# Gate products of the bidirectional layers: pairs of tiles with seven block products in place of eight, and a new order of the work around them

## The chip, the cores and the metric

The kernel runs on one core of one Trainium2 chip. The metric is the device time of one execution in microseconds. The times before are 2038.31 us as the median of three runs (2038.30 to 2046.05).

## The reference

The program is two stacks one after the other on 512 tokens of width 1024. What matters here is the end of each of the two layers of the second stack (`second_block`):

```python
h = _rms_norm(x, norm_g[l]); p = h @ w_in[l]
c_q, c_kv, k_pe, z_a, u_f, z_f, g_a, g_f = _split_in(p)        # g_a and g_f: 1024 columns each
o_a = _mla_branch(...)                                           # attention, 512 wide
y_a = (o_a * jax.nn.silu(z_a)) @ w_attn_proj[l]
y_f = (_fourier_branch(u_f) * jax.nn.silu(z_f)) @ w_fourier_proj[l]
m = (jax.nn.sigmoid(g_a + b_merge[l, 0]) * y_a
     + jax.nn.sigmoid(g_f + b_merge[l, 1]) * y_f)
x = x + m @ w_out[l]
```

## The kernel before, in words

Activations lie feature-major: a tile is 128 features by 512 tokens, eight tiles (`KT`) make the width. Every float32 product is made of three matmuls on split operands, `w_hi*x_lo + w_lo*x_hi + w_hi*x_hi` (helper `three`, matmuls at L870 to L872), so one 128-wide output tile over eight input tiles is 24 matmuls of 512 columns.

Weights come as a stream of 312 blocks of 128 x 1024 numbers (eight 128 x 128 tiles, 512 KB). `block` says which product uses which block. A block passes through: SP loads it into `raw` (three slots, `RING`), ScalarE rounds it to `w_hi` (L1594), GpSimd computes `w_lo = raw - w_hi` (L3113), TensorE uses it. ScalarE issues the rounding at places written out by hand in its program: `passed(key)` and `product(key)` call `weights(b + 2)`, where b is the key's last block. Each engine's program is written out in order; nothing is reordered at run time. PSUM has eight banks; `bank_filled`, `bank_read` and `block_used` hand them from TensorE to VectorE and ScalarE and back.

The multilayer perceptrons of the first stack already use seven products for eight (`seven`, matmuls at L975 to L977). The 1024 x 512 product of a pair of output tiles is cut in 2 x 2 blocks. From a weight block VectorE forms four sums of 128 x 256 (`weight_sums`, L2379 to L2384) in banks 4 and 5, after ScalarE has copied one quarter there (`w21`, L1610). ScalarE rounds the sums (L1621), VectorE subtracts (`weight_sums_lo`, L2390). Sums of the inputs (`t_hi`, `t_lo`) are formed once per layer. Half a pair, one block, is then 42 matmuls of 256 columns. Seven outputs of VectorE (L2466 to L2478) put the pair's two tiles together.

The end of a bidirectional layer, which changes, runs like this in the kernel before:

- TensorE: attention, then eight small products of the Fourier branch (`dd`, L1499 to L1502), then the products `f` (two blocks, four output banks, 48 matmuls). Then for m = 0 to 7: gate tile `ga` m, gate tile `gf` m, one block each, and `ya2` m and `yf2` m, four input tiles each, which share a block. Then eight tiles `out2`.
- VectorE: `d_lo` (L3028) for the eight `dd`; `of` g = `f` g * `z_f` (L3034) and its low part (`lo`, L2316), g = 0 to 3; for each m the gates times the norm's root (L3042), two products with the sigmoids (L3046), their sum (L3049) and its low part.
- ScalarE: `d_hi` (L2246), the silu of `z_f` (L2248), the rounding of two weight blocks, the high parts of `of` (L1683), then sigmoids (L2257) and weight blocks in turns.

Of the kernel before, what the change touches and what calls it, by code (L numbers as in the profile page):

```python
# [27 lines left out]
P = 128  # L28
T = 512
# [108 lines left out]
def stream_of(inp):  # L138
# [76 lines left out]
    for l in range(LAYERS2):  # L215
# [147 lines left out]

def plan_core():
# [62 lines left out]
    def mlp(layer):  # L427
# [8 lines left out]
        for part in range(1, FF_PARTS + 1):  # L436
            for g in range(2):
# [12 lines left out]
                for m in range(NT * g, NT * g + NT, 2):  # L450
# [78 lines left out]
    for l in range(LAYERS2):  # L529
# [29 lines left out]
        splits(*[("of", l, g) for g in range(FG)])
        for m in range(KT):  # L560
            each("ga", l, m, n=1)
            each("gf", l, m, n=1)
            gemm([("ya2", l, m), ("yf2", l, m)], 1, apart=True)
            splits(("m", l, m))
        each("out2", l, n=KT)
    sums = [block[key][0] + n for key in block if key[0] == "up" for n in range(2)]
# [7 lines left out]
def place(nc, c):  # L574
# [133 lines left out]
    c.m_hi, _ = put("m_hi", [P, KT, T], o, F32R)  # L708
    c.m_lo, _ = put("m_lo", [P, KT, T], o + 16384, F32R)
# [16 lines left out]
    c.sig, _ = put("sig", [P, 4, T], local)  # L726
# [4 lines left out]
    assert o <= tail, o - tail  # L731
    c.u_f, _ = put("u_f", [P, 4, T], a + 16384 + 8192)


def add_semaphores(nc, ctx, c):
# [26 lines left out]
    c.split_src = sem("split_src")  # L762
    c.split_hi = sem("split_hi")
# [75 lines left out]
def program_tensor(pe, nc, c, block, bank, split, beside, early, sum_blocks):  # L839
# [101 lines left out]
    def seven(layer, part, g, half):  # L941

        key, first = ("up", layer, part, g), (part, g) == UP_PAIRS[0]
# [4 lines left out]
        for n, (_, w, x) in enumerate(SEVEN):  # L948
            bnk, use, _ = bank[(*key, n // 2)]
            if half == 0 and n % 2 == 0:  # L950
                if use:
                    pe.wait_ge(c.bank_read[bnk], use)
                if first:
                    pe.wait_ge(c.split_lo, split[("a", layer, int(bnk < 2), bnk)] + 1)
                elif bnk % 2 == 0:
                    before = ("a", layer, part, bnk // 2) if g else ("a", layer, part - 1, 2 + bnk // 2)
                    pe.wait_ge(c.split_lo, split[before] + 1)
            out = c.psum[bnk][:, n % 2 * HALF:n % 2 * HALF + HALF]
            for k in range(2):
                i = 2 * half + k  # L960
                if first and x < X_11:
                    pe.wait_ge(c.split_lo, split[("t", 2 * layer + 1, i)] + 1)
# [17 lines left out]
            elif half and n % 2:  # L980
                ins.then_inc(c.bank_filled[bnk], 1)
# [2174 lines left out]
```

## Time and profile before

| what | value |
|---|---|
| median of three runs | 2038.31 us |
| profiled execution | 2038.94 us |
| its span, first to last instruction | 2037.0 us |
| TensorE busy | 2020.0 us, 99% |
| VectorE busy | 1166.9 us, 57% |
| ScalarE busy | 1007.8 us, 49% |
| GpSimd busy | 730.5 us, 36% |
| DMA | 179.19 MB, mean 88 GB/s |
| granted TensorE clock | 1.0 |

The profiled execution's span is its time but for 1.9 us around it. Busy time of TensorE is that of matmuls whose ends are modelled, and a matmul's shown duration overlaps the next one's start; what a matmul costs in a full stream is the distance between two starts. The same holds in part for VectorE and ScalarE: their instructions follow each other a little faster than they last.

### The profile page before, as it was taken

The numbers are of one execution on the slowest core, as the hardware profiler recorded it, in microseconds if no ns is written. First come the engines' busy times: TensorE is split into PE (matmuls) and PEld (weight loads), VectorE is DVE, ScalarE is ACT, GpSimd is POOL, SyncE is SP. The second block draws the span as 40 slices with busy tenths as digits, with TensorE's granted clock in tenths as the row PEclk, the third lists the DMA queues.
The fourth block names the chain that finished last, engine by engine and source line by source line (L and its number), as shares of the span: only waits on it lengthen the run. The fifth ranks groups of instructions, "written<-read, shape, count | busy, mean of one in ns | idle before, by whom it ended". The sixth has DMA issues, their size and how long they took to land.

```text
span 2037.0 us, 30204 instructions
## 1 busy us (share of the span) xinstructions
PE 2020.0 (99%) x12180; PEld 1663.9 (82%) x12180; DVE 1166.9 (57%) x1983; ACT 1007.8 (49%) x1655; POOL 730.5 (36%) x342
## 2 busy tenths in 40 slices
PE   8999999999999999999999999999999999999999
PEld 6777788989888886778898888878788887878887
DVE  6884566666647158863656564667733334774331
ACT  7752465444436328874544343566743344775221
POOL 3332144444444631004444444434044443402443
PEclk9999999999999999999999999999999999999999
DMA  4432123332232430002333232222022232201222
GB/s 160 133 131 72 47 97 104 103 104 96 103 104 91 145 96 32 1 16 93 104 104 104 100 108 94 93 80 87 2 93 93 95 101 84 83 22 63 93 97 89
DMA packets 62729, 179.19 MB, mean 88 GB/s; under 512 B 17776, under 2 KB 18160, under 8 KB 62592
## 3 DMA queue, kind: packets, MB, share of 16 engines
q1 hardware_dynamic: 47600, 168.04, 24.3%
q10 hardware_dynamic: 14992, 9.22, 1.7%
q8 instruction: 98, 1.61, 0.3%
q14 instruction: 39, 0.32, 0.0%
HBM read 171.97 MB, written 3.70 MB: 86 GB/s over the span
## 4 chain that ended last, share of the span: by engine, by line
PE 97%; ACT 1%; DVE 1%; issue 0%; DMA 0%; POOL 0%; DVEq 0%; ACTq 0%
PE banks L870 23%; PE banks L872 22%; PE banks L871 22%; PE banks L977 4%; PE banks L976 4%; PE banks L975 4%; PE banks L1362 2%; PE banks L1328 2%; PE banks L1341 2%; PE banks L1451 1%; PE banks L1464 1%; PE banks L1436 1%; PE banks L921 1%; PE banks L1442 1%; PE banks L1044 1%; PE banks L1236 1%
## 5 line engine op out<-in xcount | busy, mean ns | idle before, releaser
L3113 POOL TENSOR_TENSOR w_lo<-raw,w_hi 128x1024 fp32r<-128x1024 f32 (+4 forms) x338 | 730.3, 2165 | 1290.5 <-ACT w_hi L1594 1190.9
L1594 ACT ACTIVATE w_hi<-raw 128x1024 fp32r<-128x1024 f32 (+2 forms) x286 | 284.4, 994 | 453.6 <-PE banks L872 334.7
L870 PE MATMUL banks<-h_lo,w_hi 128*128 128x512 f32 (+1 forms) x992 | 401.0, 404 | 7.5 <-POOL w_lo L3113 7.5
L872 PE MATMUL banks<-h_hi,w_hi 128*128 128x512 f32 (+1 forms) x992 | 387.8, 391 | 0.0
L871 PE MATMUL banks<-h_hi,w_lo 128*128 128x512 f32 (+1 forms) x992 | 387.6, 391 | 0.0
L870 PE MATMUL banks<-a_lo,w_hi 128*128 128x512 f32 x768 | 304.4, 396 | 0.0
L872 PE MATMUL banks<-a_hi,w_hi 128*128 128x512 f32 x768 | 299.2, 390 | 0.0
L871 PE MATMUL banks<-a_hi,w_lo 128*128 128x512 f32 x768 | 299.2, 390 | 0.0
L2362 DVE TENSOR_TENSOR x<-x,banks 128x512 f32<-128x512 f32 x168 | 115.1, 685 | 213.4 <-PE banks L872 213.4
L870 PEld LDWEIGHTS banks<-h_lo,w_hi 128*128 128x128 f32 (+1 forms) x992 | 186.0, 187 | 54.4 <-POOL w_lo L3113 7.5
L871 PEld LDWEIGHTS banks<-h_hi,w_lo 128*128 128x128 f32 (+1 forms) x992 | 186.2, 188 | 41.8 <-issue 5.5
L872 PEld LDWEIGHTS banks<-h_hi,w_hi 128*128 128x128 f32 (+1 forms) x992 | 186.0, 187 | 40.9 <-issue 1.2
L870 PEld LDWEIGHTS banks<-a_lo,w_hi 128*128 128x128 f32 x768 | 144.1, 188 | 36.9 <-DVE x L2362 7.4
L872 PEld LDWEIGHTS banks<-a_hi,w_hi 128*128 128x128 f32 x768 | 144.2, 188 | 30.9
L871 PEld LDWEIGHTS banks<-a_hi,w_lo 128*128 128x128 f32 x768 | 144.2, 188 | 29.1 <-issue 1.0
L2390 DVE TENSOR_TENSOR w_lo_s<-banks,w_hi_s 128x1024 fp32r<-128x1024 f32 x52 | 63.5, 1220 | 88.8 <-ACT w_hi_s L1621 88.8
L2257 ACT ACTIVATE sig<-sig,params 128x512 f32<-128x512 f32 x32 | 23.1, 723 | 135.6 <-DVE sig L3042 135.6
L975 PE MATMUL banks<-t_lo,w_hi_s 128*128 128x256 f32 x312 | 86.1, 276 | 0.0
L976 PE MATMUL banks<-t_hi,w_lo_s 128*128 128x256 f32 x312 | 86.1, 276 | 0.0
L977 PE MATMUL banks<-t_hi,w_hi_s 128*128 128x256 f32 x312 | 86.1, 276 | 0.0
L3042 DVE TENSOR_TENSOR sig<-banks,norm 128x512 f32<-128x512 f32 x32 | 22.1, 692 | 104.1 <-PE banks L872 104.1
L1621 ACT ACTIVATE w_hi_s<-banks 128x1024 fp32r<-128x1024 f32 x52 | 52.9, 1018 | 35.7 <-DVE banks L2384 35.7
(423 smaller groups left out, 3760.0 us busy)
## 6 DMA issues: line engine op xcount, KB each, us to landing
raw<-in_weights SPq DMA_DIRECT2D x311, 512.0 KB, 3.2
x<-in_x SPq DMA_DIRECT2D x4, 512.0 KB, 5.9
AT<-row_dram ACTq DMA_DIRECT2D x4, 512.0 KB, 8.7
out<-x SPq DMA_DIRECT2D x8, 256.0 KB, 2.2
eg<-row_dram ACTq DMA_DIRECT2D x8, 128.0 KB, 3.1
phase<-in_phase ACTq DMA_DIRECT2D x1, 706.0 KB, 4.0
phase<-in_phase ACTq DMA_DIRECT2D x1, 704.0 KB, 4.2
ld_dram<-Ld ACTq DMA_DIRECT2D x1, 512.0 KB, 4.5
```

Source lines behind the costliest of these rows:

```text
L870: mm(out, w_hi, x_lo, start=first, stop=False)
L871: mm(out, w_lo, x_hi, start=False, stop=False)
L872: return mm(out, w_hi, x_hi, start=False, stop=last)
L975: mm(out, w_hi, x_lo, start=half == k == n % 2 == 0, stop=False, skip_group_check=True)
L976: mm(out, w_lo, x_hi, start=False, stop=False, skip_group_check=True)
L977: ins = mm(out, w_hi, x_hi, start=False, stop=half == k == 1, skip_group_check=True)
L1328: mm(halves[s], q[r, j, qt * P:end], k[r, both, j // 4, 0:end], start=n == 0, stop=False)
L1594: ins = f(c.w_hi[:, b % RING, cols], c.raw[:, b % RING, cols], ACT.Copy)
L1621: f(c.w_hi_s[:, i % 2, :], c.pairs[SUM_BANKS[0] // 2][:, :, :].rearrange("p b t -> p (b t)"), ACT.Copy).then_inc(c.s_hi_ready, 1)
L2362: tt_op(c.x[:, m, :], c.x[:, m, :], out[:, :], ALU.add).then_inc(release(key), 1)
L2390: tt_op(c.w_lo_s[:, i % 2, :], c.pairs[SUM_BANKS[0] // 2][:, :, :].rearrange("p b t -> p (b t)"), c.w_hi_s[:, i % 2, :].bitcast(F32), ALU. ...
L3113: return nc.gpsimd.tensor_tensor(c.w_lo[:, slot, to], c.raw[:, slot, first:end], c.w_hi[:, slot, to].bitcast(F32), ALU.subtract)
```

## The change

The gates of a bidirectional layer are computed branch by branch: eight attention gates with their `y` products first, then eight Fourier gates with theirs. Only the first two attention gate tiles (`ga` 0 and 1) stay plain. The other fourteen gate tiles of a layer are seven pairs (`GATE_PAIRS`), each two blocks of 42 matmuls of 256 columns. After each pair comes one block for its two `y` tiles. The number of weight blocks stays 312; 28 blocks more than before are used through sums (80 instead of 52).

New work per layer:

- `inputs(i)`, i = 0 to 3: ScalarE copies a quarter tile of `h_hi` into a PSUM bank, VectorE makes the four sums of the inputs with nine instructions of 256 columns (h_hi and h_lo are added apart), ScalarE rounds them (`inputs_hi`), VectorE subtracts (`inputs_lo`). Inputs 0 and 1 stand between the `dd` and the `of` products, 2 and 3 behind the `of` products.
- The sums of the weights for 14 blocks, as in the perceptrons; seven instructions per pair for the outputs (`pair_outputs`).
- The sum of the branches goes through PSUM: the attention product waits in `gated`, the Fourier product is multiplied and added in its bank, ScalarE takes its high part and VectorE its low part from there.

The core of the diff (`...` marks what is left out):

```diff
+GATE_PAIRS = [(branch, p) for branch in range(2) for p in range(PAIRS)][1:]
+GATE_INPUT_BANKS = [(6, 7), (4, 5), (6, 7), (6, 7)]
...
# plan_core
+    def gates(l):
+        for m in range(2):
+            key, b = ("ga", l, m), at_blocks(1)
+            block[key] = (b, b)
+            take(key, m, False)
+        merged(l, 0, 0, 2)
+        for branch, p in GATE_PAIRS:
+            key = ("gate", l, branch, p)
+            block[key] = (at_blocks(2), 0)
+            for b in range(4):
+                take((*key, b), b, b < 3)
+            merged(l, branch, p, DOWN_BANKS[0])
...
# program_tensor
+        for m in range(2):
+            gemm(("ga", l, m), h_hi, h_lo)
+        merged(0, 0)
+        for n, (branch, p) in enumerate(GATE_PAIRS):
+            for half in range(2):
+                seven(("gate", l, branch, p), half, [c.t2_hi[:, i] for i in range(PAIRS)], c.t2_lo, (c.w_hi_g, c.w_lo_g),
+                      ready=None if n else ("t2", l))
+            merged(branch, p)
         for m in range(KT):
-            gemm(("ga", l, m, 0), h_hi, h_lo)
-            gemm(("gf", l, m, 0), h_hi, h_lo)
-            gemm(("ya2", l, m), a_hi[0:4], a_lo[0:4], needs=parted("oa", l) if m == 0 else None)
-            gemm(("yf2", l, m), a_hi[4:8], a_lo[4:8], tile0=4, needs=parted("of", l) if m == 0 else None)
...
# program_scalar
+        inputs(0)
+        inputs(1)
         read(("zf", l, 3))
         f(c.z_f[:, :, :], c.z_f[:, :, :], ACT.Silu).then_inc(c.z_ready, 1)
+        inputs_hi(0)
+        inputs_hi(1)
         for g in range(FG):
             product(("f", l, g))
             hi(("of", l, g), c.a_hi[:, 4 + g, :], after=("f", l, g))
...
+        inputs(2)
+        inputs_hi(2)
+        passed("ga", l, 0)
+        read(("ga", l, 0))
+        gate(0, 0)
+        inputs(3)
+        w21(first_pair)
+        inputs_hi(3)
+        passed("ga", l, 1)
...
# program_vector
+        def inputs(i):
...
+            after(marked(tt_op(d[:, right], d[:, right], low_1[:, right], ALU.add)))
+            t1 = marked(tt_op(d[:, left], d[:, right], high_1[:, left], ALU.subtract))
+            t3 = marked(tt_op(d[:, right], high_2[:, right], d[:, right], ALU.subtract))
+            after(t1)
+            t1 = marked(tt_op(d[:, left], d[:, left], low_1[:, left], ALU.subtract))
+            after(t3)
+            tt_op(d[:, right], d[:, right], low_2[:, right], ALU.add)
+            after(t1)
+            after(marked(tt_op(b[:, left], high_2[:, right], d[:, left], ALU.subtract)))
+            after(marked(tt_op(b[:, left], b[:, left], low_2[:, right], ALU.add)))
+            after(marked(tt_op(b[:, right], high_2[:, left], b[:, left], ALU.subtract)))
+            tt_op(b[:, right], b[:, right], low_2[:, left], ALU.add).then_inc(c.t_ready, 1)
...
+        inputs(0)
+        inputs(1)
+        inputs_lo(0)
+        inputs_lo(1)
         dve.wait_ge(c.z_ready, 2 * l + 2)
         for g in range(FG + 1):
...
+        inputs(2)
+        gate_rooted(0, 0, ("ga", l, 0))
+        inputs_lo(2)
+        inputs(3)
+        weight_sums(first_pair)
+        inputs_lo(3)
+        gate_rooted(0, 1, ("ga", l, 1))
+        weight_sums_lo(first_pair)
+        gated(0, 0)
+        weight_sums(first_pair + 1)
+        gated(0, 1)
+        weight_sums_lo(first_pair + 1)
+        for n, (branch, p) in enumerate(GATE_PAIRS):
...
+            if ahead:
+                weight_sums(at + 3)
+            if branch and p:
+                merged_lo(2 * p - 2)
+                merged_lo(2 * p - 1)
+            if ahead:
+                weight_sums_lo(at + 3)
+            pair_outputs(key, (2 * len(UP_PAIRS)) + l * len(GATE_PAIRS) + n, c.first_g[:, n % 2, :], [c.part_g[:, i, :] for i in range(3)])
+            for i in range(2):
+                read((*key, 2 * i + 1))
+                gate_rooted(branch, 2 * p + i, (*key, 2 * i), c.psum[2 * i])
+            if ahead:
+                weight_sums(at + 4)
+            gated(branch, 2 * p)
+            if ahead:
+                weight_sums_lo(at + 4)
+            gated(branch, 2 * p + 1)
```

Where the instructions stand. VectorE, from the last of attention to the `of` products of the first bidirectional layer, before (`d_lo` low parts of the Fourier products, `stage<-banks,z_f` the `of` products, `a_lo` their low parts):

```order
L3028 TENSOR_TENSOR d_lo<-banks,d_hi 128x256 x8
L3034 TENSOR_TENSOR stage<-banks,z_f 128x512 x2
L2316 TENSOR_TENSOR a_lo<-stage,a_hi 128x512
L3034 TENSOR_TENSOR stage<-banks,z_f 128x512
L2316 TENSOR_TENSOR a_lo<-stage,a_hi 128x512
L3034 TENSOR_TENSOR stage<-banks,z_f 128x512
L2316 TENSOR_TENSOR a_lo<-stage,a_hi 128x512 x2
L3042 TENSOR_TENSOR sig<-banks,norm 128x512 x2
```

And VectorE at the same place now, from the second group of nine sums of the inputs:

```order
L3199 TENSOR_TENSOR banks<-h_hi,banks 128x256
L3200 TENSOR_TENSOR banks<-banks,h_lo 128x256
L3201 TENSOR_TENSOR banks<-h_hi,banks 128x256
L3202 TENSOR_TENSOR banks<-banks,h_lo 128x256
L3208 TENSOR_TENSOR t_lo<-banks,t_hi 128x1024 x2
L3244 TENSOR_TENSOR stage<-banks,z_f 128x512 x2
L2464 TENSOR_TENSOR a_lo<-stage,a_hi 128x512
L3244 TENSOR_TENSOR stage<-banks,z_f 128x512
L2464 TENSOR_TENSOR a_lo<-stage,a_hi 128x512
L3244 TENSOR_TENSOR stage<-banks,z_f 128x512
L2464 TENSOR_TENSOR a_lo<-stage,a_hi 128x512 x2
L3191 TENSOR_TENSOR banks<-banks,h_lo 128x256
```

Between `d_lo` and the `of` products there stand 20 more instructions now, and the nine sums of inputs 2 follow the last low part.

ScalarE at the same place, before (`w_hi` are weight blocks, `a_hi` the high parts of `of`, `sig` a sigmoid):

```order
L2246 ACTIVATE d_hi<-banks 128x256 x8
L2248 ACT_TABLE_LOAD
L2248 ACTIVATE z_f<-z_f 128x2048
L1594 ACTIVATE w_hi<-raw 128x1024 x2
L1683 ACTIVATE a_hi<-stage 128x512 x4
L1594 ACTIVATE w_hi<-raw 128x1024
L2257 ACT_TABLE_LOAD
L2257 ACTIVATE sig<-sig,params 128x512
```

And ScalarE now (`t_hi` rounds the sums of the inputs, `gated` holds a sigmoid, the 1024 columns into `w_hi_g` are the sums of the first block of the first pair):

```order
L2344 ACTIVATE banks<-h_hi 128x256 x2
L2365 ACT_TABLE_LOAD
L2365 ACTIVATE z_f<-z_f 128x2048
L2349 ACTIVATE t_hi<-banks 128x1024 x2
L1680 ACTIVATE w_hi<-raw 128x1024 x2
L1771 ACTIVATE a_hi<-stage 128x512 x4
L2344 ACTIVATE banks<-h_hi 128x256
L2349 ACTIVATE t_hi<-banks 128x1024
L1680 ACTIVATE w_hi<-raw 128x1024
L2355 ACT_TABLE_LOAD
L2355 ACTIVATE gated_165<-gated_165,params 128x512
L2344 ACTIVATE banks<-h_hi 128x256
```

The two weight blocks behind `f` (those of `ga` 0 and of the block after it) now stand behind the rounding of both input sums.

## Rows read from the trace of the kernel before

**Rows 1.** The page, first part: busy time and share of each engine.

```profile
PE 2020.0 (99%) x12180; PEld 1663.9 (82%) x12180; DVE 1166.9 (57%) x1983; ACT 1007.8 (49%) x1655; POOL 730.5 (36%) x342
```

**Rows 2.** Busy time by stretch: a gate stage, and perceptron pairs (PE, PEld, DVE, ACT, POOL).

```profile
1488.39:1618.95 130.56, 130.56 (x577) 108.14 (x576) 45.50 (x48) 41.30 (x50) 58.48 (x24) 1.00 0.28 97
337.00:620.00 283.00, 283.00 (x1773) 252.32 (x1772) 171.91 (x328) 120.77 (x190) 119.64 (x67) 1.00 0.31 103
```

**Rows 3.** Waits of PE over the whole span: total, times, longest.

```profile
PE banks L870 <- POOL w_lo L3113: 7.5, 1, 7.5
PE banks L1328 <- ACT prob L2103: 1.3, 2, 0.9
```

**Rows 4.** Timeline of PE (start, duration): first matmuls of two plain gate blocks.

```profile
1488.39 0.39 PE L870 MATMUL banks<-h_lo,w_hi 128*128 128x512 f32 x1
...
1493.83 0.39 PE L870 MATMUL banks<-h_lo,w_hi 128*128 128x512 f32 x1
```

**Rows 5.** Timeline of PE: first matmul of half a perceptron pair, and of what follows.

```profile
421.70 0.28 PE L975 MATMUL banks<-h_lo,w_hi 128*128 128x256 f32 x1
...
426.46 0.40 PE L870 MATMUL banks<-a_lo,w_hi 128*128 128x512 f32 x1
```

**Rows 6.** Timeline of DVE, end of the Fourier products of the first bidirectional layer.

```profile
1476.77 1.77 DVE L3028 TENSOR_TENSOR d_lo<-banks,d_hi 128x256 fp32r<-128x256 f32 x4 [0.22 <-ACT d_hi L2246]
...
1488.18 0.68 DVE L2316 TENSOR_TENSOR a_lo<-stage,a_hi 128x512 fp32r<-128x512 f32 x1
1488.78 0.68 DVE L3034 TENSOR_TENSOR stage<-banks,z_f 128x512 f32<-128x512 f32 x1
```

**Rows 7.** Timeline of ACT, the same layer: silu, table load and sigmoid.

```profile
1479.39 1.92 ACT L2248 ACTIVATE z_f<-z_f 128x2048 f32<-128x2048 f32 x1
...
1491.16 1.28 ACT L2257 ACT_TABLE_LOAD   x1
1494.76 0.72 ACT L2257 ACTIVATE sig<-sig,params 128x512 f32<-128x512 f32 x1 [2.32 <-DVE sig L3042]
```

**Rows 8.** Timeline of DVE in a perceptron pair: three of four weight sums.

```profile
418.53 0.43 DVE L2379 TENSOR_TENSOR banks<-raw,banks 128x256 f32<-128x256 f32 x1 [0.74 <-ACT banks L1610]
418.87 0.42 DVE L2380 TENSOR_TENSOR banks<-banks,raw 128x256 f32<-128x256 f32 x1
419.33 0.43 DVE L2382 TENSOR_TENSOR banks<-banks,raw 128x256 f32<-128x256 f32 x1
```

**Rows 9.** The groups of the page: the low part of the weight sums.

```profile
L2390 DVE TENSOR_TENSOR w_lo_s<-banks,w_hi_s 128x1024 fp32r<-128x1024 f32 x52 | 63.5, 1220 | 88.8 <-ACT w_hi_s L1621 88.8
```

**Rows 10.** Timeline of ACT in a perceptron pair.

```profile
418.13 0.37 ACT L1610 ACTIVATE banks<-raw 128x256 f32<-128x256 f32 x1
...
422.92 1.01 ACT L1621 ACTIVATE w_hi_s<-banks 128x1024 fp32r<-128x1024 f32 x1
...
426.72 0.63 ACT L1591 ACTIVATE w_hi<-raw 128x512 fp32r<-128x512 f32 x1 [1.05 <-PE banks L977]
```

**Rows 11.** Timeline of POOL: a whole weight block in the gate stage.

```profile
1491.22 2.39 POOL L3113 TENSOR_TENSOR w_lo<-raw,w_hi 128x1024 fp32r<-128x1024 f32 x1 [4.10 <-ACT w_hi L1594]
```

**Rows 12.** Timeline of POOL in a perceptron pair: a block used through sums.

```profile
427.73 2.00 POOL L3113 TENSOR_TENSOR w_lo<-raw,w_hi 128x512 fp32r<-128x512 f32 x2 [2.23 <-ACT w_hi L1594]
```

**Rows 13.** Timeline of POOL, one block later in the gate stage.

```profile
1522.43 2.54 POOL L3113 TENSOR_TENSOR w_lo<-raw,w_hi 128x1024 fp32r<-128x1024 f32 x1 [1.77 <-ACT w_hi L1594]
```

**Rows 14.** Timeline of DVE at the moment of rows 13.

```profile
1522.63 2.89 DVE L2316 TENSOR_TENSOR m_lo<-stage,m_hi 128x512 fp32r<-128x512 f32 x1
```

**Rows 15.** Timeline of POOL before attention: two blocks back to back.

```profile
1377.60 5.21 POOL L3113 TENSOR_TENSOR w_lo<-raw,w_hi 128x1024 fp32r<-128x1024 f32 x2 [4.74 <-ACT w_hi L1594]
```

**Rows 16.** Timeline of DVE at the moment of rows 15.

```profile
1378.39 4.96 DVE L2968 TENSOR_TENSOR k_pe<-kpe,k_root 32x512 f32<-32x512 f32 x2
```

**Rows 17.** Timeline of PE at the start of the program, first and fourteenth matmul.

```profile
7.51 0.65 PE L870 MATMUL banks<-h_lo,w_hi 128*40 128x512 f32 x1 [7.51 <-POOL w_lo L3113]
...
13.08 0.59 PE L871 MATMUL banks<-h_hi,w_lo 128*40 128x512 f32 x1
```

More of the change, by code:

```diff
@@ L456, in mlp, with merged @@
                         take(key, DOWN_BANKS[i], i == 0)
+    def merged(l, branch, p, first_bank):
+        keys = [("y", l, branch, 2 * p + i) for i in range(2)]
+        early.add(keys[0])
+        b = at_blocks(1)
+        for i, key in enumerate(keys):
+            block[key] = (b, b)
+            if branch:
+                bank[key] = (first_bank + i, uses[first_bank + i], fills[first_bank + i])
+                fills[first_bank + i] += i == 0
+            else:
+                take(key, first_bank + i, i == 0)
+    def gates(l):
+        for m in range(2):
+            key, b = ("ga", l, m), at_blocks(1)
+            block[key] = (b, b)
+            take(key, m, False)
[6 more added lines that the diff above has]
+            merged(l, branch, p, DOWN_BANKS[0])
     norm(0)
@@ L557, in plan_core @@
                 scratch("dd", l, g, k)
+        for b in range(4, 8):
+            beside[("gates", l, b)] = uses[b]
         gemm([("f", l, g) for g in range(FG)], FK, apart=True)
[L559 to L564, printed above, removed]
+        splits(("t2", l, 0), ("t2", l, 1), *[("of", l, g) for g in range(FG)], ("t2", l, 2), ("t2", l, 3))
+        gates(l)
+        splits(*[("m", l, m) for m in range(KT)])
         each("out2", l, n=KT)
-    sums = [block[key][0] + n for key in block if key[0] == "up" for n in range(2)]
+    sums = [block[key][0] + n for kind in ("up", "gate") for key in block if key[0] == kind for n in range(2)]
     return block, bank, split, beside, early, at, sums
@@ L939, in program_tensor, with seven @@
     a_hi, a_lo = tiles(c.a_hi), tiles(c.a_lo)
-    def seven(layer, part, g, half):
-        key, first = ("up", layer, part, g), (part, g) == UP_PAIRS[0]
+    def seven(key, half, t_hi, t_lo, w_sums, free=None, ready=None):
         b = block[key][0] + half
@@ L952, in seven @@
                     pe.wait_ge(c.bank_read[bnk], use)
[L953 to L957, printed above, removed]
+                if free:
+                    free(bnk)
             out = c.psum[bnk][:, n % 2 * HALF:n % 2 * HALF + HALF]
@@ L960, in seven @@
                 i = 2 * half + k
-                if first and x < X_11:
-                    pe.wait_ge(c.split_lo, split[("t", 2 * layer + 1, i)] + 1)
+                if ready and x < X_11:
+                    pe.wait_ge(c.split_lo, split[(*ready, i)] + 1)
                 if w < 4:
@@ L981, in seven, with up_pair, free @@
                 ins.then_inc(c.bank_filled[bnk], 1)
+    def up_pair(layer, part, g):
+        first = (part, g) == UP_PAIRS[0]
+        def free(bnk):
+            if first:
+                pe.wait_ge(c.split_lo, split[("a", layer, int(bnk < 2), bnk)] + 1)
+            elif bnk % 2 == 0:
+                before = ("a", layer, part, bnk // 2) if g else ("a", layer, part - 1, 2 + bnk // 2)
+                pe.wait_ge(c.split_lo, split[before] + 1)
+        for half in range(2):
+            seven(("up", layer, part, g), half, [c.t_hi[:, i] for i in range(PAIRS)], [c.t_lo[:, i] for i in range(PAIRS)],
+                  (c.w_hi_s, c.w_lo_s), free, ("t", 2 * layer + 1) if first else None)
     def down(layer, part, g):
@@ L1003, in mlp @@
                 elif part < FF_PARTS:
-                    seven(layer, part, g, 0)
-                    seven(layer, part, g, 1)
+                    up_pair(layer, part, g)
                 down(layer, part - 1, g)
```

211 lines of the change are left out of this document (151 added, 60 removed).

## The prediction

> **What bounds the kernel now.** I read the page's busy times first. TensorE (PE) is busy for 2020.0 of 2037.0 us, VectorE (DVE) for 57% and ScalarE (ACT) for 49% [rows 1]. Then the busy time by stretch: in the gate stage of the first bidirectional layer PE is busy for all of its 130.56 us, and in 283 us of perceptron pairs, which already use seven products, for all 283 us, with DVE at 171.91 us [rows 2]. Then PE's waits: apart from 7.5 us at the very start no line waited over 1.3 us in total [rows 3]. So PE's column stream is the time of this kernel. A column saved is time saved, and a wait of PE adds in full, because there is no older wait for it to hide in. The last thing I read were the timelines of DVE, ACT and GpSimd (POOL) around the gate stage, since the change gives them much new work there.
>
> **What the change removes.** A plain block is 24 matmuls of 512 columns and takes 1493.83 - 1488.39 = 5.44 us [rows 4]. Half a pair is 42 matmuls of 256 columns and takes 426.46 - 421.70 = 4.76 us [rows 5], exactly 7/8. So 0.68 us are saved per block. Per layer 14 blocks change, 28 in both: 28 x 0.68 = 19.0 us. The `y` and `out2` blocks keep their matmuls. That is the most the change can give.
>
> **What it adds on PE.** Nothing is added as work, but three waits at the start of the stage. I follow the first layer in the trace's own times; the second layer runs the same list. Prices from rows: a dependent DVE instruction of 256 columns starts 0.46 us after its forerunner, an independent one 0.34 us [rows 8]; one of 512 columns 0.60 us after [rows 6]; a low part of 1024 columns 1.22 us [rows 9]; ACT 0.37 us for 256 columns, 1.01 for 1024, 0.63 for 512 [rows 10]; POOL 2.4 us for a whole block [rows 11], 2.0 for one used through sums [rows 12].
>
> One `inputs` is nine DVE instructions, four of them waiting for the one right before: 4 x 0.46 + 4 x 0.33 = 3.2 us from the first start to the ninth, 3.6 to its end, 3.5 to the next instruction.
>
> - DVE ends its last `d_lo` at 1476.77 + 1.77 = 1478.5 [rows 6]; ACT's copy makes it 1479.0. Inputs 0 and 1 end at 1482.6 and 1486.1. The silu (1.92 us [rows 7], its table load before it) ends about 1482.5, so it is hidden. ACT rounds the second sums until 1487.1.
> - Only then does ACT round the weight block of `ga` 0: 1488.1; POOL 1490.6. Before, that block was ready long ago. PE is free for it at 1488.39 [rows 4].
> - DVE takes the low part of inputs 1 until 1488.4, then `of` 0 and 1, and is ready for the low part of `of` 0 at 1489.7. This instruction reads two operands in SBUF while POOL works on `ga` 0's block. Such an instruction here does not run beside POOL: one that began 0.20 us after a POOL block took 2.89 us in place of 0.68 and ended 0.55 us after the block's end, 1524.97 [rows 13, 14], the normal 0.68 is in [rows 6]. So it ends at 1490.6 + 0.55 = 1491.1. `of` 2 follows, until 1491.8. It frees bank 0, which `ga` 0 now uses (in the kernel before it used the bank of `f` 0). PE starts `ga` 0 at 1491.8, 3.4 us late.
> - POOL's next block stands right behind; with two back to back two such DVE instructions took 4.96 us and the blocks 5.21 [rows 15, 16], so the second block lasts some 2.8 us, to 1493.4, and the low part of `of` 1 ends at 1493.9. `of` 3 and two more low parts: DVE is free at 1495.9.
> - Inputs 2 end at 1499.4, ACT rounds them until 1500.5, then rounds the block of the first `y` until 1501.4 and POOL until 1503.9. PE has finished `ga` 0 and 1 at 1491.8 + 10.9 = 1502.7: 1.2 us of waiting.
> - ACT goes on with a table load, 1.28, a sigmoid, 0.72 [rows 7], and the copy for inputs 3: 1503.7. DVE has nothing to do meanwhile. Inputs 3 to 1507.3; the weight sums of the first pair, four instructions, to 1508.95; ACT rounds them, 1510.0, and the two pieces of the block, 1510.9; POOL 2.0 us: 1512.95. PE starts the first pair at 1513.0.
>
> Without waits PE would start it at 1488.39 + 3 x 5.44 = 1504.7. The loss is 8.3 us (3.4, 1.2 and 3.6), 16.6 us for both layers. The block of the pair's second half comes out of POOL at 1517.8, just when PE wants it (1513.0 + 4.76): nothing, or some tenths.
>
> The Trainium skill has this blocking: "SBUF — State Buffer", section "Who interferes with whom", says that VectorE and GpSimd share a pair of ports, and that a VectorE instruction with two inputs in SBUF and a GpSimd instruction that reads SBUF exclude each other for their whole length. The trace agrees (2.89 us, above). By that page the new sums, each with one operand in PSUM, are free of it; no row of before shows these sums beside POOL's blocks but the perceptron's weight sums, which kept their 0.43 us.
>
> **The pairs after that.** A pair and its `y` block take PE 2 x 4.76 + 5.44 = 14.96 us, against 2 x 4.76 + 2 x 5.44 = 20.4 in the perceptron, so DVE has less room. In the Fourier half DVE starts per pair: 8 weight sums (3.2 us), two low parts (2.3), 7 outputs (2.5), two gates times the root (1.3), two products and two sums, each sum waiting (2.7), two low parts of `m` (1.2): 13.2 of 14.96 us; in the attention half 10.7. The longest chain: PE fills the third bank at 9.0 us of the pair; the outputs are done at 10.8, the gates times the root at 12.0, the weight sums of the second half of the next pair at 13.6, ACT's rounding at 14.6 and of the block at 15.5, POOL at 17.4. PE wants it at 14.96 + 4.76 = 19.7. 2.3 us are left, so I take zero, with the rows of the perceptron as the near case [rows 2]. The sums of `m` that PE waits for (rounded and subtracted within about 5 us of the next pair, wanted at 9.5) and the end (low part of `m` 7 about 3 us after the last `y`, wanted by the first `out2` after 4.8) are covered too. The order of branches and the bank sum cost nothing on PE. The removed sum of two SBUF tiles and the low parts of `m` that were blocked by POOL were beside PE and give nothing.
>
> **Sum.** -19.0 + 16.6 = -2.4 us on the profiled execution's 2038.94 us: 2036.5. It was 0.6 above the median of the runs, so the forecast is 2036.0. Bounds of the loss per layer: 5.9 us if the low parts of `of` are not blocked (2.4 less), some 9.5 if each handover costs 0.1 us more over a dozen of them. That gives 2031 to 2038.5; the forecast case's own range is 2033 to 2038.5.
>
> **Rivals.**
>
> - *No blocking between DVE and POOL there.* DVE's low parts might fall into gaps. Loss 5.9 us per layer, -7.2 in all: 2031. The rows speak for the blocking, but a shift of half a microsecond changes which instruction meets which block.
> - *The start is covered, the full gain comes.* 2038.3 - 19.0 = 2019.3. For it: the perceptron's start with the same kind of sums shows no wait [rows 3]. Against it: there six plain tiles of 5.44 us and `down` products cover the preparation, here three blocks, 16.3 us, against DVE work of 29 us between 1479 and 1508.
> - *The clock falls in the new waits.* At the start of the program the first 14 matmuls stood (13.08 - 7.51) / 13 = 0.43 us apart, the gate blocks' 0.227 [rows 17, 4]: half clock, and each such spell costs 14 x 0.20 = 2.8 us. After the start no row shows a wait of PE above 0.9 us, so the trace can't tell whether 3.4 and 3.6 us are enough. With all four long waits: 2036 + 11 = 2047. The Trainium skill, "TensorE: Matmul & The Clock Gate", Part 1, says that an idle TensorE is put back to half clock and has to earn the full one again; by it this case would come out at that time, or part of it, if these waits count as idle.
> - *Slower: the pair's chain through DVE, ACT and POOL becomes the bound.* It decides from 2.3 us more than I worked out. If each of the 12 prepared pairs (six per layer) came 2 us late, 24 us would be added: 2060. For it: DVE has 13.2 of 14.96 us filled in the Fourier half. Against it: the same chain gave no wait in 283 us of perceptron [rows 2].
>
> **Chances.** Forecast case 0.57; no blocking 0.15; full gain 0.06; clock 0.12; pair's chain 0.10. The range 2027 to 2045 leaves out the full gain, the pair's chain and the worst of the clock, about 0.2. A change under 0.5%, 10.2 us, is what a measurement of this kernel can't tell from none. Faster by more (under 2028.1): the full gain and the part of "no blocking" with a still shorter chain, 0.12. Slower by more (above 2048.5): the pair's chain and a little of the clock, 0.12. Within: 0.76.
>
> **What would show it.** In the changed kernel's profile halves of pairs 4.76 us apart; PE waits per layer of about 3.4 us before the first matmul of `ga` 0 (ended by DVE's `of` 2, or by POOL), about 1 us before the first `y`, about 3.6 us before the first pair (ended by POOL), and none beyond tenths between pairs; low parts of `of` 0 and 1 lasting over 1 us beside POOL's blocks; matmuls of 512 columns 0.227 us apart right after each wait if the clock holds, 0.43 us if it fell. I am wrong if PE waits in every pair, if the first pair starts less than 6 or more than 10 us late, or if a chain I left out stands before it.

## The result, and the profile after

The changed kernel takes 2040.84 us in the median of 20 runs (2039.29 to 2047.63), the kernel before 2038.30 us in its own 20 (2037.36 to 2046.05), on the same chip. The ratio is 1.0014, with a 95% interval of 1.0008 to 1.0021. So 28 more blocks go through sums, 19 us of matmuls are gone, and the kernel is 2.5 us slower. The forecast was 2036.0, a gain of 2.3 us. The time lies in the forecast range and within 0.5% of before, but on the other side of it.

The page of the changed kernel, its first part (engine, busy us, share of the span, instructions), to be read against [rows 1]:

```profile
span 2039.0 us, 31708 instructions
PE 2008.8 (99%) x12684; PEld 1676.6 (82%) x12684; DVE 1287.2 (63%) x2301; ACT 1055.8 (52%) x1755; POOL 716.3 (35%) x356
```

PE is busy 11.2 us less than before, not 19.0, and the span is 2.0 us longer (2037.0 before). So about 13 us went into waits, and some PE time came back as slower matmuls. PE's waits (line that waited, its releaser: total us, times, longest), to be read against [rows 3]:

```profile
PE banks L931 <- POOL w_lo L3344: 7.9, 1, 7.9
PE banks L931 <- DVE stage L3244: 5.9, 2, 3.2
PE banks L1032 <- POOL w_lo L3344: 5.5, 2, 3.4
PE banks L1400 <- ACT prob L2191: 1.3, 2, 0.9
PE banks L931 <- issue: 1.1, 1, 1.1
```

The first and fourth rows were there before. The three others, 12.5 us, are new, and they are the three places of the prediction: before `ga` 0 (released by the `of` products, L3244), before the first `y` (1.1 us, in the second layer only) and before the first pair (L1032, released by POOL). No row names a wait between pairs.

PE's timeline at the five restarts (start, duration; in brackets the idle time before it and the releaser):

```profile
1491.33 0.79 PE L931 MATMUL banks<-h_lo,w_hi 128*128 128x512 f32 x1 [3.25 <-DVE stage L3244]
...
1512.70 0.38 PE L1032 MATMUL banks<-h_lo,w_hi 128*128 128x256 f32 x1 [2.07 <-POOL w_lo L3344]
...
1863.59 0.50 PE L931 MATMUL banks<-h_lo,w_hi 128*128 128x512 f32 x1 [2.65 <-DVE stage L3244]
...
1875.86 0.47 PE L931 MATMUL banks<-a_lo,w_hi 128*128 128x512 f32 x1 [1.10 <-issue]
...
1884.98 0.39 PE L1032 MATMUL banks<-h_lo,w_hi 128*128 128x256 f32 x1 [3.41 <-POOL w_lo L3344]
```

The first pair starts at 1512.70, where the prediction had 1513.0 (`f` begins 0.51 us earlier in this profile than in that of before, 1476.91 against 1477.42). And the busy time by stretch (PE, PEld which is TensorE's loading of weights, DVE, ACT, POOL; behind them the granted clock, the DMA share and GB/s), to be read against [rows 2]: `ga` 0 and 1 with what lies before the first `y`, the first pair of each layer, the second pair of the first layer with its `y` block, and three narrow stretches:

```profile
1491.33:1505.02 13.69, 13.69 (x48) 11.05 (x49) 10.84 (x20) 6.10 (x9) 3.97 (x2) 0.79 0.25 85
1512.70:1524.23 11.53, 11.53 (x85) 11.53 (x85) 6.74 (x14) 5.77 (x9) 5.24 (x3) 0.85 0.40 139
1884.98:1896.52 11.54, 11.54 (x85) 11.54 (x86) 6.75 (x14) 5.78 (x9) 5.24 (x3) 0.85 0.42 138
1529.68:1544.70 15.02, 15.02 (x110) 14.06 (x108) 10.42 (x22) 7.11 (x12) 6.29 (x4) 1.00 0.33 106
1490.00:1497.00 7.00, 5.67 (x13) 4.46 (x14) 6.81 (x11) 1.54 (x3) 2.90 (x2) 0.52 0.42 150
1514.00:1517.50 3.50, 3.50 (x20) 3.50 (x19) 2.45 (x5) 2.79 (x4) 1.85 (x2) 0.52 0.32 119
1886.00:1889.60 3.60, 3.60 (x20) 3.60 (x19) 2.55 (x5) 2.98 (x4) 1.81 (x1) 0.53 0.43 142
```

The first three rows show what the kernel before had nowhere in this stage [rows 2]: a granted clock of 0.79 and 0.85. In the narrow stretches it is half. It fell to its lower level (1.2 of 2.4 GHz) three times: at 1490.2 for 6.8 us, in the wait before `ga` 0; at 1514.1 for 3.4 us, 1.4 us after the first pair had started; at 1886.2 for 3.4 us, 1.2 us after the second layer's first pair had started. The two halves of a first pair last 11.53 and 11.54 us, those of the second pair 9.55 (1529.68 to 1539.23): 1.98 us more each. The falls are not those of one execution alone: the mean granted clock of the 20 executions of the changed kernel is 0.994 to 0.998, while 18 of 21 executions of the kernel before, on the chip of the first four experiments, have 0.999 or 1.0.

The balance against the kernel before, from the first matmul of `f` to the end of the gate stage, in us of the two profiles:

| | layer 1 | layer 2 |
|---|---|---|
| first pair starts later by | 8.49 | 7.89 |
| halves of the first pair longer by | 1.98 | 1.98 |
| 14 blocks, each 0.68 shorter | -9.52 | -9.52 |
| `y` and gate blocks each 0.02 slower than priced | 0.4 | 0.4 |
| sum | 1.35 | 0.75 |
| measured, the stage's length | +1.35 | +0.80 |

Together 2.15 us, and the span grew by 2.0.

### The profile page after: what moved, and what is told of

It is laid out like the page before. It is cut to its first block, busy times and chain, and to the rows that moved or that the text cites. A ratio compares the mean times of both kernels' runs of the same rounds, so it can differ in the third digit from the quotient of the medians.

```text
span 2039.0 us, 31708 instructions
## 1 busy us (share of the span) xinstructions
PE 2008.8 (99%) x12684; PEld 1676.6 (82%) x12684; DVE 1287.2 (63%) x2301; ACT 1055.8 (52%) x1755; POOL 716.3 (35%) x356
## 4 chain that ended last, share of the span: by engine, by line
PE 93%; DVE 3%; ACT 2%; issue 1%; POOL 0%; DMA 0%; ACTq 0%; DVEq 0%
PE banks L931 19%; PE banks L933 19%; PE banks L932 19%; PE banks L1032 6%; PE banks L1034 6%; PE banks L1033 6%; PE banks L1434 2%; PE banks L1400 2%; PE banks L1413 2%; PE banks L1523 1%; PE banks L1536 1%; PE banks L1508 1%; PE banks L982 1%; PE banks L1514 1%; PE banks L1116 1%
## 5 line engine op out<-in xcount | busy, mean ns | idle before, releaser
L931 PE MATMUL banks<-h_lo,w_hi 128*128 128x512 f32 (+1 forms) x768 | 315.0, 410 | 13.8 <-POOL w_lo L3344 7.9
L932 PE MATMUL banks<-a_hi,w_lo 128*128 128x512 f32 x832 | 324.5, 390 | 0.0
L933 PE MATMUL banks<-h_hi,w_hi 128*128 128x512 f32 (+1 forms) x768 | 301.4, 392 | 0.0
L932 PE MATMUL banks<-h_hi,w_lo 128*128 128x512 f32 (+1 forms) x768 | 301.1, 392 | 0.0
L931 PEld LDWEIGHTS banks<-h_lo,w_hi 128*128 128x128 f32 (+1 forms) x768 | 144.5, 188 | 52.6 <-POOL w_lo L3344 7.9
L932 PEld LDWEIGHTS banks<-h_hi,w_lo 128*128 128x128 f32 (+1 forms) x768 | 144.7, 188 | 33.3 <-issue 5.3
L933 PEld LDWEIGHTS banks<-h_hi,w_hi 128*128 128x128 f32 (+1 forms) x768 | 144.4, 188 | 32.4 <-issue 1.0
L1032 PE MATMUL banks<-h_lo,w_hi 128*128 128x256 f32 x320 | 89.0, 278 | 5.5 <-POOL w_lo L3344 5.5
L1034 PE MATMUL banks<-h_hi,w_hi 128*128 128x256 f32 x320 | 89.2, 279 | 0.0
L1033 PE MATMUL banks<-h_hi,w_lo 128*128 128x256 f32 x320 | 89.0, 278 | 0.0
L1032 PE MATMUL banks<-t_lo,w_hi_s 128*128 128x256 f32 x312 | 86.1, 276 | 0.0
```

What stands on the lines that cost most here:

```text
L931: mm(out, w_hi, x_lo, start=first, stop=False)
L932: mm(out, w_lo, x_hi, start=False, stop=False)
L933: return mm(out, w_hi, x_hi, start=False, stop=last)
L1032: mm(out, w_hi, x_lo, start=half == k == n % 2 == 0, stop=False, skip_group_check=True)
L1033: mm(out, w_lo, x_hi, start=False, stop=False, skip_group_check=True)
L1034: ins = mm(out, w_hi, x_hi, start=False, stop=half == k == 1, skip_group_check=True)
```

## The experiments

Theory A: the work ahead of the first pair (a chain of VectorE, then ScalarE, then GpSimd) makes PE wait 8.3 us per layer as predicted, and the clock falls behind these waits, which costs the other 2 us per layer. Rivals are named in the expectations. `...` marks lines left out of an edit. The first four kernels ran on one chip, with the kernel before at 2038.91 us there (21 runs), the last two on another, with it at 2038.51 (9 runs). The changed kernel did not run again beside them: a difference to its 2040.84 us is one between two measurements, a ratio to the kernel before is not.

### Busy: dummy matmuls in PE's waits

```diff
...
+        keep_busy(6, 15).then_inc(c.kept_busy, 1)     # 15 matmuls of 512 columns into an idle bank
         for m in range(2):
             gemm(("ga", l, m), h_hi, h_lo)
...
+        keep_busy(3, 4)
         merged(0, 0)
...
+        keep_busy(0, 15)
         for n, (branch, p) in enumerate(GATE_PAIRS):
```

> The changed kernel with matmuls of no use in the three places where TensorE waits (per layer 15 before ga 0, 4 before the first y, 15 before the first pair, 512 columns each, into banks that are free then). The output is the same. Theory A (what the forecast left out is the clock, which falls after the long waits and makes the first pair last 11.5 us in place of 9.6): the first pairs start where they did (1512.7 and 1885.0, each within 0.5 us), last 9.6 us, the granted clock is 1.0 from the first to the last layer, and the time is 2 x 2.0 = 4 us less, about 2037, with less spread between executions. Theory B (the first pair is long because its second half's weights or sums come late from VectorE, ScalarE or GpSimd): the first pair still lasts about 11.5 us and the time stays 2041.

Measured: 2038.16 us (2036.77 to 2040.93, 11 runs), ratio to before 0.9993 [0.9984, 1.0002]. The span is 2035.3 us, 3.7 below the changed kernel's. The two stretches of the start, busy time and clock as above:

```profile
1487.00:1525.00 38.00, 37.74 (x205) 32.10 (x204) 31.41 (x58) 18.86 (x30) 15.93 (x9) 1.00 0.27 85
1858.00:1895.00 37.00, 36.98 (x204) 31.77 (x203) 30.49 (x57) 17.86 (x28) 15.73 (x9) 1.00 0.27 86
```

PE is busy for nearly all of it and the clock stays at 1.00. The two halves of a first pair last 10.00 us in both layers in place of 11.53 and 11.54. That is 1.54 us less, but not the 9.6 us that Theory A expected. The first row is Busy's first pair in the first layer, the second that of the kernel of Order only (below), where PE comes to the pair without any wait or dummy before it:

```profile
1512.31:1522.31 10.00, 10.00 (x85) 10.00 (x85) 6.63 (x13) 5.79 (x9) 4.95 (x3) 1.00 0.48 157
```

```profile
1510.10:1519.66 9.56, 9.56 (x86) 9.55 (x84) 7.19 (x13) 5.07 (x9) 3.22 (x2) 1.00 0.35 112
```

Both have the full clock. In Busy the pair's first matmul stands 0.22 us ahead of the next and the matmuls of its second half start 0.118 us apart, in Order only 0.113. The changed kernel's first pairs have the same 0.118 in their second halves. So of the 1.98 us that a first pair lasts longer, 1.54 are the clock's (at the lower level its matmuls start 0.213 us apart) and 0.44 come at the full clock, with the late start of the pair. What makes these matmuls slower no run shows.

The first pair itself starts 0.14 and 0.11 us later than in the changed kernel, since the dummies hold PE a little; from `f` to the end of the stage the layers are 1.40 and 1.43 us shorter than the changed kernel's, which is 1.54 less these. The other 0.9 us of the 3.7 lie outside the gate stages (0.5 before the first, 0.3 between the two) and are no effect of the edit that I can name. So matmuls that nobody reads make the changed kernel faster, by 2.7 us of median, or 3.3 if each is taken against the kernel before that ran beside it: they give back the clock's part and nothing else, and the preparation takes as long as it did. Against the kernel before Busy can't be told from equal.

### Early: the weight blocks of `ga` 0 and 1 rounded first, `f` in other banks

```diff
# plan_core
+        turn[0] += 2
         gemm([("f", l, g) for g in range(FG)], FK, apart=True)
+        turn[0] += 2
# program_scalar
         inputs(0)
+        weights(block[("ga", l, 0)][0])
         inputs(1)
...
         inputs_hi(0)
+        weights(block[("ga", l, 1)][0])
         inputs_hi(1)
```

> The changed kernel with the weight blocks of ga 0 and ga 1 rounded ahead of the input sums' roundings on ScalarE, and with the f products in banks 0 to 3 in order, so that ga 0 waits for of 0 and not for of 2. Theory A (the start of the stage is one chain of VectorE and ScalarE, lengthened by low parts of of that are blocked beside GpSimd): the first wait goes from 3.4 to about 0.7 us, the low parts of of 0 and 1 last 0.7 us as GpSimd is idle then, the chain is 2.6 us shorter, the first pair starts 2.6 us earlier in each layer, and the time is 5 us less, about 2035.5; the wait before the first pair grows to about 5 us. Theory B (only the first wait matters): the whole first wait of 3.4 and 3.0 us is won: 6.4 us and the clock's part. Theory C (the chain's end is not moved by the blocking): the first pair starts at the same time and 2041 stays.

Measured: 2037.67 us (2034.23 to 2041.87, 11 runs), 0.9993 [0.9984, 1.0002]; span 2036.5. PE's restarts in the first layer and the last one of the second:

```profile
1489.59 0.50 PE L933 MATMUL banks<-h_lo,w_hi 128*128 128x512 f32 x1 [0.60 <-DVE stage L3248]
...
1502.32 0.47 PE L933 MATMUL banks<-a_lo,w_hi 128*128 128x512 f32 x1 [1.56 <-issue]
...
1511.43 0.39 PE L1034 MATMUL banks<-h_lo,w_hi 128*128 128x256 f32 x1 [3.42 <-POOL w_lo L3348]
...
1881.50 0.58 PE L1034 MATMUL banks<-h_lo,w_hi 128*128 128x256 f32 x1 [3.42 <-POOL w_lo L3348]
```

The wait before `ga` 0 is down from 3.25 to 0.60 us, and the first pair comes 6.28 and 5.66 us late, in place of 8.49 and 7.89. The last wait is now 3.42 us in both layers and not the 5 us of the expectation, because PE also waits before the first `y` (1.56 and 1.54 us). The clock falls behind both last waits. The two halves of the first pairs:

```profile
1511.43:1522.95 11.52, 11.52 (x84) 11.52 (x85) 6.75 (x14) 5.78 (x9) 5.23 (x3) 0.85 0.44 139
1881.50:1894.11 12.61, 12.61 (x85) 12.61 (x85) 6.75 (x14) 5.78 (x9) 5.24 (x3) 0.77 0.41 127
```

They last 11.52 and 12.61 us in place of 9.55. In the second layer the clock was down for 6.8 us, and 1.1 us of the 4.4 us won on the waits went back to it. The median is 3.2 us below the changed kernel's, less than expected, because the falls stayed. VectorE's low part of `of` 0, which lasted 1.32 us beside GpSimd's block in the changed kernel, has its normal length here, and so has that of `of` 1 (0.68):

```profile
1490.29 0.69 DVE L2468 TENSOR_TENSOR a_lo<-stage,a_hi 128x512 fp32r<-128x512 f32 x1 [0.16 <-ACT a_hi L1773]
```

The two were blocked for 0.64 and 1.57 us, 2.21 together, and the first pair comes 2.21 and 2.23 us earlier. So the blocking was worth its own length on the way to the first pair. The wait before `ga` 0 shrank by more, and there the other banks of `f` have a part that this run doesn't separate. What is left, 6.28 and 5.66 us, lies behind VectorE's work for the first pair; the next run tests that.

### Order only: the first pair's weight sums ahead of inputs 2 and 3

```diff
# program_vector
+        weight_sums(first_pair)
         inputs(2)
+        weight_sums_lo(first_pair)
         gate_rooted(0, 0, ("ga", l, 0))
         inputs_lo(2)
+        weight_sums(first_pair + 1)
         inputs(3)
-        weight_sums(first_pair)
+        gate_rooted(0, 1, ("ga", l, 1))
+        gated(0, 0)
+        weight_sums_lo(first_pair + 1)
+        gated(0, 1)
         inputs_lo(3)
-        gate_rooted(0, 1, ("ga", l, 1))
-        weight_sums_lo(first_pair)
-        gated(0, 0)
-        weight_sums(first_pair + 1)
-        gated(0, 1)
-        weight_sums_lo(first_pair + 1)
```

ScalarE's copies and roundings move with them, and its sigmoids and their table load come later.

> The changed kernel with another order behind the of products: the weight sums of the first pair come first, inputs 2 and 3, which only the pair's second half reads, after them, and the weight blocks are rounded as soon as their sums are, the sigmoid with its table load later. Theory A (the last wait is the chain through inputs 2 and 3 and the table load): the wait before the first pair (2.2 and 3.6 us) is gone or below 0.5 us, the first wait (3.4 and 3.0) stays, the clock falls at most once per layer, and the time is 2030 to 2032. Theory B (VectorE's total work is what is too much for 16.3 us, in any order): the wait moves into the pair, before its second half or its banks, and the time is above 2036.

Measured: 2030.87 us (2029.75 to 2034.01, 5 runs), 0.9959 [0.9946, 0.9972]; span 2028.9. From the waits of the whole span:

```profile
PE banks L931 <- POOL w_lo L3345: 7.9, 1, 7.9
PE banks L931 <- DVE stage L3245: 6.0, 2, 3.3
```

Only the waits before `ga` 0 are left, 3.27 and 2.68 us. The same instructions in another order are worth 10 us of median. The clock fell behind both, 3.4 us each time, and here it can be priced, as nothing behind `ga` 0 and 1 absorbs it: the two last 12.64 and 12.46 us. They take 10.88 us in the kernel before and 11.01 in the next run, behind a wait and at the full clock, so the fall itself costs 1.63 and 1.44 us. (It fell a third time, at 776 us; the next run has such a fall too.)

### Both edits together

> Both edits together. Theory A: per layer one wait of about 0.7 us before ga 0 and none over 0.5 us after it, clock 1.0 throughout, all pairs 15.0 us apart: -19.0 us for the matmuls, +1.4 for the two waits, +0.8 for pairs of 15.02 in place of 14.96 us: 2021.5. Theory B (VectorE's work is too much in any order): waits of 2 us or more remain in the first pair, 2026 or more.

Measured: 2024.42 us (2023.85 to 2026.87, 5 runs), 0.9923 [0.9909, 0.9936]: 14.5 us faster than before, and some 16 faster than the changed kernel. PE's restarts in the first layer, and one in the second:

```profile
1491.73 0.50 PE L933 MATMUL banks<-h_lo,w_hi 128*128 128x512 f32 x1 [0.60 <-DVE stage L3249]
...
1510.12 0.39 PE L1034 MATMUL banks<-t_lo,w_hi_g 128*128 128x256 f32 x1 [0.38 <-DVE gated L3222]
...
1873.78 0.39 PE L1034 MATMUL banks<-t_lo,w_hi_g 128*128 128x256 f32 x1 [0.38 <-DVE gated L3222]
```

What is left is 0.60 us before `ga` 0 and 0.38 in the first pair, which waits for a bank that VectorE still reads (gate times the norm's root, L3222). The whole of the gate stage runs at the full clock (first row), but a stretch of the first stack's attention does not (second row):

```profile
1486.00:1620.00 134.00, 133.01 (x877) 121.06 (x876) 104.60 (x206) 68.39 (x104) 55.97 (x33) 1.00 0.32 103
770.00:790.00 20.00, 18.20 (x115) 11.38 (x115) 13.18 (x26) 10.82 (x34) 0.00 (x0) 0.74 0.01 1
```

There the clock was down for 10.2 us from 776.1 on. From the same matmul to the first of `f` (775.59 to 1479.98) this profile needs 704.4 us and the changed kernel's (775.91 to 1476.91), with no fall there, 701.0: 3.4 us that are no part of the change. The profiled execution was the slowest of the five, 2026.87 us; the other four took 2023.85 to 2025.06, still 2.3 us or more above what was expected. From `f` to its end the stage of the two layers is 134.34 and 133.72 us, 7.20 and 7.85 less than before (141.54 and 141.57), where 9.1 would be the full gain with the slightly slower pairs. So 1.9 and 1.2 us are lost where the expectation had 0.7 each, which is 1.7 of the missing 2.3 or more; 0.97 of each is the first pair, with its wait and with the slower matmuls behind it that Busy showed. The rest is open.

### Short sums: the input sums on 8 columns

```diff
-            left, right = slice(0, HALF), slice(HALF, T)
+            left, right = slice(0, 8), slice(HALF, HALF + 8)
```

> The changed kernel in which the nine VectorE instructions of each of the four input sums work on 8 columns in place of 256 (the input sums are incomplete). By the prediction's working each of the nine costs 0.33 to 0.46 us, 3.5 us per group; with 8 columns some 0.1 to 0.2 us each are left, so a group is 1.7 to 2.5 us shorter and the four on VectorE's path 7 to 10 us. Theory A (the start of the stage hangs on VectorE's chain of input sums, then ScalarE and GpSimd; and the clock falls in the waits): the wait before ga 0 drops from 3.4 us to about 0 to 1, the one before the first pair from 3.4 to 3.8 us to about 0 to 1.5 us, falls of the clock become rare, and the time is 2022 to 2029 us. Rival (the waits are set by ScalarE's order of roundings or by GpSimd's blocks and not by VectorE's sums): waits stay within 1 us of what they are and the time is 2036 to 2041 us.

Measured: 2024.07 us (2023.38 to 2024.36, 5 runs), 0.9921 [0.9905, 0.9937]; span 2022.3, the clock at 1.00 throughout. VectorE at the ninth instruction of inputs 0, the first of inputs 1, and the waiting low part of `of`:

```profile
1480.63 0.17 DVE L3202 TENSOR_TENSOR banks<-banks,h_lo 128x8 f32<-128x8 f32 x1
1480.71 0.16 DVE L3191 TENSOR_TENSOR banks<-banks,h_lo 128x8 f32<-128x8 f32 x1
...
1487.54 1.15 DVE L2464 TENSOR_TENSOR a_lo<-stage,a_hi 128x512 fp32r<-128x512 f32 x1 [0.16 <-ACT a_hi L1771]
...
1489.21 2.27 DVE L2464 TENSOR_TENSOR a_lo<-stage,a_hi 128x512 fp32r<-128x512 f32 x1
```

A group takes 1.33 us from its first instruction (1479.38) to the next group's first, in place of 3.53, and the four groups on the path are 8.8 us shorter. PE then waits 0.46 us before `ga` 0 and 0.40 before the first pair. ScalarE's and GpSimd's work and order are the changed kernel's, so it is VectorE's chain of input sums that the start hangs on. The blocking stays (1.15 and 2.27 us for instructions of 0.68) and costs PE next to nothing.

### Waits ladder: when does the clock fall?

```diff
# program_tensor of the kernel before
+        pe.wait_ge(c.delayed, l * KT + m + 1)
         gemm(("ga", l, m, 0), h_hi, h_lo)
# program_scalar
+        act.wait_ge(c.block_used, block[("ga", l, m, 0)][0])
+        for n in range(DELAYS[l][m]):      # [1..8] in the first layer, [8..1] in the second
+            ins = f(c.sq[:, 0, :], c.x[:, 0, :], ACT.Copy)
...
+        ins.then_inc(c.delayed, 1)
```

> The kernel before, in which TensorE is made to wait once ahead of each gate tile ga m (every 16.3 us) for a chain of 1 to 8 ScalarE copies of 512 columns: 1 to 8 of them in the first layer, 8 to 1 in the second. Waits of about 0.6 to 5.5 us, 16 in all, some 50 us together; the sum of the waits is added to the span in any case. Theory A (a wait of about 3 us and more, or the TensorE activity just before and after it, makes the granted clock fall to half for some microseconds): falls behind the waits of about 3 us and more, none behind those under 2 us; each fall of 3.4 us costs 3.4 / 2 = 1.7 us of TensorE's work where it lies in work, less where part of it lies in a wait. Theory C (the fall does not hang on the length of the wait but on something else, a phase): falls behind some of the long waits and not others, or behind short ones, and differently in the two layers at one length. Theory B (the loss in the changed kernel has nothing to do with the granted clock): no falls here at any length.

Measured: 2123.17 us (one run), span 2121.4, mean clock 0.983. PE's waits for the chain were 51.4 us in 16 places. Between two waits stand the same 72 matmuls. The restarts after the first, second, third and fifth wait of the first layer, and after the fifth of the second:

```profile
1493.23 0.50 PE L872 MATMUL banks<-h_lo,w_hi 128*128 128x512 f32 x1 [2.18 <-ACT sq L2258]
...
1511.22 0.50 PE L872 MATMUL banks<-h_lo,w_hi 128*128 128x512 f32 x1 [1.38 <-ACT sq L2258]
...
1529.88 0.79 PE L872 MATMUL banks<-h_lo,w_hi 128*128 128x512 f32 x1 [2.04 <-ACT sq L2258]
...
1572.10 0.80 PE L872 MATMUL banks<-h_lo,w_hi 128*128 128x512 f32 x1 [3.36 <-ACT sq L2258]
...
1980.07 0.58 PE L872 MATMUL banks<-h_lo,w_hi 128*128 128x512 f32 x1 [3.36 <-ACT sq L2258]
```

And the work behind the same five waits (stretch, its length, busy times, then the clock):

```profile
1493.00:1509.40 16.40, 16.17 (x71) 13.42 (x72) 2.46 (x4) 5.75 (x7) 7.18 (x3) 1.00 0.19 64
1511.00:1527.40 16.40, 16.18 (x71) 13.43 (x72) 2.43 (x4) 4.99 (x7) 7.19 (x3) 1.00 0.25 86
1529.80:1547.60 17.80, 17.72 (x71) 14.54 (x72) 2.23 (x4) 4.84 (x7) 7.16 (x3) 0.90 0.19 64
1572.00:1590.80 18.80, 18.70 (x71) 15.25 (x72) 2.08 (x3) 4.86 (x7) 7.17 (x3) 0.85 0.17 57
1980.00:1997.90 17.90, 17.83 (x71) 14.58 (x72) 2.08 (x3) 4.83 (x7) 7.17 (x3) 0.90 0.16 59
```

All 16 waits, with PE's work behind each (16.2 us at the full clock):

| wait, us | times | clock fell | work behind it longer by, us |
|---|---|---|---|
| 0.72, 1.38 | 3 | never | 0 |
| 2.04, 2.18 | 3 | 2 of 3, for 3.4 us | 1.6 (and 0) |
| 2.70 | 2 | both, 3.4 us | 1.4, 1.5 |
| 3.36 | 2 | both, once 6.8, once 3.4 us | 2.6, 1.6 |
| 4.03 to 4.69 | 4 | all, 6.8 us | 2.5 to 2.9 |
| 5.35, 6.80 | 2 | both, 6.8 us | 2.4, 2.3 |

The rival without falls (B) is out. In this run no wait up to 1.4 us brought a fall and every one from 2.7 us on did; around 2 us something else decides too (C): a wait of 2.18 us was left alone and two of 2.04 were not. One more wait, of 2.3 us at 197 us, stands in this profile and in no other here; it is none of the 16, and the clock fell 1.3 us after its restart, for 3.4 us. Part of a fall often lies in the wait itself, which is why 6.8 us at half speed cost 2.3 to 2.9 us and not 3.4.

## Why the prediction missed

- *The gain, 0.68 us per block.* Right. The halves of later pairs are 4.78 us long each (9.55 together) and a `y` block 5.47, 0.02 to 0.03 more than the 4.76 and 5.44 of [rows 4, 5], so a pair with its `y` block takes 15.02 and not 14.96 us. Over a layer that is 0.4 us, which the sum did not have.
- *The start of the stage, 8.3 us per layer.* Right in size: 8.49 and 7.89 us, with `ga` 0 late by 3.44 and 2.82 us (predicted 3.4). Short sums showed that it hangs on VectorE's nine instructions per group. The middle wait of 1.2 us came only in the second layer (1.10). In the first `ga` 0 and 1 lasted 13.69 us at the half clock, which ate it and shortened the last wait to 2.07 us.
- *The blocking, 2.4 us of it.* Seen, 2.21 us. VectorE (start, duration) and GpSimd in the changed kernel, to be read against [rows 13 to 16]:

```profile
1489.36 1.32 DVE L2464 TENSOR_TENSOR a_lo<-stage,a_hi 128x512 fp32r<-128x512 f32 x1 [0.16 <-ACT a_hi L1771]
1490.60 0.68 DVE L3244 TENSOR_TENSOR stage<-banks,z_f 128x512 f32<-128x512 f32 x1
1491.20 2.25 DVE L2464 TENSOR_TENSOR a_lo<-stage,a_hi 128x512 fp32r<-128x512 f32 x1
```

```profile
1487.77 5.13 POOL L3344 TENSOR_TENSOR w_lo<-raw,w_hi 128x1024 fp32r<-128x1024 f32 x2 [67.69 <-ACT w_hi L1680]
```

The second blocked instruction ends at 1493.45, 0.55 us after GpSimd's block (1492.90), the very number of [rows 13, 14]. The rule of the Trainium skill, "SBUF — State Buffer", "Who interferes with whom", fits these rows, as does its other side: `of` 2, with one operand in PSUM, kept its 0.68 us in the midst of it.

- *The pairs' chain, zero.* Right: no wait between pairs in either layer, with VectorE busy for 10.42 of 15.02 us in the attention half.
- *The clock, zero in the sum.* This is the step that failed. The prediction said that "the trace can't tell whether 3.4 and 3.6 us are enough", priced a fall at 2.8 us after each of four waits, gave it 0.12, and left it out of the likeliest case. Measured: falls behind three of the four long waits. One came in a wait of 3.25 us, and the later waits absorbed its cost; two began inside the first pairs and cost 1.54 us each, 3.1 us in all. Busy took these away, and in the ladder each of the eight waits from 3.36 us on brought a fall. So the clock case was the likely one, at under a third of the price that I gave it: 3 us, not 11. The Trainium skill, "TensorE: Matmul & The Clock Gate", Part 1, says that an idle TensorE is put back to half clock. These falls agree with it.
- *The matmuls of a first pair at the full clock.* The sum had them at their old price. They cost 0.44 us more per first pair, 0.9 in all. With -19.0, +16.4, +3.1, +0.9 and +0.8 (the pairs and `y` blocks of the first point) the sum is +2.2; the span changed by 2.0.

The two large terms, -19.0 and +16.4, nearly cancel, so small ones give the sign. Without the clock's 3.1 us the sum is -0.9: the clock turned it, and Busy, with the clock held, has a median 0.8 us below the kernel before. The chance of 0.12 for the clock was too low for a mechanism that the same trace showed at the program's start [rows 17].

## What to carry to other kernels

Where TensorE is the bound and never waits, a new wait of some 2 us or more cost itself and mostly 1.4 to 2.9 us of half-speed matmuls behind it, so put both in the sum. When a faster form of a product needs preparation, count the preparation for the first use against the plain work that covers it, and order it by what the first use needs first: here nearly the same instructions in another order, with the `f` products in other banks, turned a loss of 2.5 us into a gain of 14.5. When nothing can fill a wait, dummy matmuls kept the clock up here, and they were worth 2.7 us of median.

## What the runs showed of the hardware

- A fall can begin after TensorE is back at work: 1.4 and 1.2 us after the restart of the first pairs in the changed kernel, when the first matmuls had already run at the full rate.
- Of two waits of the same 3.36 us one cost 6.8 us at the lower clock and the other 3.4. Why wasn't tested. Nor was why the wait of 2.65 us in the changed kernel's second layer brought no fall when 2.68 and 2.70 us elsewhere did.
- The clock can fall without any such wait: in three of the eight profiles it fell in the attention of the first stack, 0.3 to 0.5 us after a gap of 0.9 us between small matmuls (for 3.4, 3.4 and 10.2 us). The other five have the same gap and no fall. The fall of 10.2 us cost 3.4 us, those of 3.4 us 0.4 or less. The kernel before isn't free of falls either: the 3 of its 21 executions that took 2042 us or more had mean clocks of 0.997 and 0.998. So part of the spread between single executions is the clock.
- Behind a wait the stream can be slower at the full clock: the 256-column matmuls in the second half of a late first pair start 0.118 us apart and not 0.113, with the clock at 1.00 (Busy, Both).
- A VectorE instruction of 8 columns still takes 0.17 us, and a dependent one starts 0.21 us after its forerunner, an independent one 0.08 to 0.13. The same two of 256 columns need 0.46 and 0.33. So some 0.2 us of a dependent instruction's price are there even at 8 columns.
